# Light expert stages spread over eight heavy blocks, and light activations turned as one block diagonal tile

## The reference

```python
def _moe(h, router, w_gate, w_up, w_down):      # cut to what matters
    logits = xf @ router
    top_logits, top_idx = lax.top_k(logits, 2)
    gates = softmax(top_logits)
    # rows of each expert, padded to blocks
    y = silu(xb @ w_gate[e]) * (xb @ w_up[e]) @ w_down[e]     # 1024 x 3584, 1024 x 3584, 3584 x 1024
    out = segment_sum(y * slot_gate, slot_tok)
```

## Time and profile before

| | us |
|---|---|
| median of 3 executions | 1515.26 (1514.31 to 1519.34) |
| the profiled execution | 1516.86 |
| its span, first to last instruction | 1515.0 |
| TensorE busy | 1476.6 (97% of the span) |
| VectorE, ScalarE, GpSimd busy | 911.1, 734.3, 302.9 |

### The profile page before, as it was taken

How to read it: one execution, slowest core, us unless ns; L and a number is a source line. 1 busy time by engine, 2 the same in 40 slices (tenths; PEclk the granted TensorE clock), 3 DMA queues, 4 the chain that set the end, 5 groups by cost and what they waited for, 6 DMA issues and landing times.

```text
span 1515.0 us, 22445 instructions
## 1 busy us (share of the span) xinstructions
PE 1476.6 (97%) x9550; PEld 1133.6 (75%) x9550; DVE 911.1 (60%) x665; ACT 734.3 (48%) x588; POOL 302.9 (20%) x295
## 2 busy tenths in 40 slices
PE   9999999999999999999999999999999999999997
PEld 8887889999998878886666666667666666666785
DVE  6555665655556866885555546555555555555686
ACT  5444455344336435774444445444444544444565
POOL 5599324500024401880000000000000000000100
PEclk9999999999999999999999999999999999999999
DMA  9645538765531164999999999999999999999993
GB/s 346 190 161 173 172 134 299 276 232 190 182 129 42 47 259 150 374 392 407 394 410 403 398 409 413 411 408 408 407 401 397 410 402 409 407 394 407 409 396 150
DMA packets 141597, 469.61 MB, mean 310 GB/s; under 512 B 8648, under 2 KB 21152, under 8 KB 129200
## 3 DMA queue, kind: packets, MB, share of 16 engines
q1 hardware_dynamic: 137424, 454.58, 78.3%
q0 software_dynamic: 3920, 13.44, 2.7%
q10 hardware_dynamic: 144, 0.07, 0.0%
HBM read 462.02 MB, written 15.21 MB: 315 GB/s over the span
## 4 chain that ended last, share of the span: by engine, by line
PE 73%; DMA 14%; DVE 6%; ACT 4%; issue 1%; POOL 1%; POOLq 0%; SPq 0%; ACTq 0%; DVEq 0%
PE PS L2066 70%; DMA weights_raw<-in_moe_w_up 8%; DVE weights_lo L1560 4%; DMA weights_raw<-in_moe_w_gate 4%; ACT weights_hi L1132 3%; PE PS L2281 1%; DMA row_back<-results_by_slot,pair_index 1%; DMA weights_raw<-in_moe_w_down 1%; POOL b_padded L950 1%; PE PS L2480 1%; ACT c_padded L1132 0%; DMA results_by_slot<-small_expert_rows 0%; DVE residual L1560 0%; DMA constants<-in_constants 0%; DVE residual L1955 0%
## 5 line engine op out<-in xcount | busy, mean ns | idle before, releaser
L1560 DVE TENSOR_TENSOR weights_lo<-weights_raw,weights_hi 128x2048 fp32r<-128x2048 f32 (+2 forms) x323 | 680.2, 2117 | 406.4 <-ACT weights_hi L1132 405.3
L1132 ACT ACTIVATE weights_hi<-weights_raw 128x2048 fp32r<-128x2048 f32 (+2 forms) x323 | 564.7, 1754 | 465.2 <-PE PS L2066 311.2
L2066 PE MATMUL PS<-weights_hi,gathered_hi 128*128 128x512 f32 (+1 forms) x640 | 240.2, 375 | 1.6 <-DVE weights_lo L1560 1.0
L2066 PE MATMUL PS<-weights_hi,gathered_lo 128*128 128x512 f32 (+1 forms) x640 | 234.5, 366 | 0.0
L2066 PE MATMUL PS<-weights_lo,gathered_hi 128*128 128x512 f32 (+1 forms) x640 | 234.2, 366 | 0.0
L2066 PE MATMUL PS<-weights_hi,act_transposed_hi 128*128 128x512 f32 x456 | 185.9, 408 | 2.3 <-DVE weights_lo L1560 2.3
L2066 PE MATMUL PS<-x_transposed_hi,weights_hi 128*128 128x256 f32 x640 | 181.2, 283 | 1.3 <-DVE weights_lo L1560 1.1
L2066 PE MATMUL PS<-weights_hi,act_transposed_lo 128*128 128x512 f32 x456 | 180.6, 396 | 0.0
L2066 PE MATMUL PS<-weights_lo,act_transposed_hi 128*128 128x512 f32 x456 | 180.0, 395 | 0.0
L2066 PE MATMUL PS<-x_transposed_hi,weights_lo 128*128 128x256 f32 x640 | 179.6, 281 | 0.0
L2066 PE MATMUL PS<-x_transposed_lo,weights_hi 128*128 128x256 f32 x640 | 179.6, 281 | 0.0
(11 more groups left out here) (330 smaller groups left out, 1453.4 us busy)
## 6 DMA issues: line engine op xcount, KB each, us to landing
weights_raw<-in_moe_w_up SPq DMA_DIRECT2D x127, 896.0 KB, 9.7
weights_raw<-in_moe_w_gate SPq DMA_DIRECT2D x125, 896.0 KB, 9.6
weights_raw<-in_moe_w_down SPq DMA_DIRECT2D x96, 1024.0 KB, 8.3
weights_raw<-in_ret_w_in SPq DMA_DIRECT2D x24, 1024.0 KB, 6.6
weights_raw<-in_moe_w_down SPq DMA_DIRECT2D x32, 512.0 KB, 9.0
weights_raw<-in_ffn_w_gate SPq DMA_DIRECT2D x14, 1024.0 KB, 5.1
weights_raw<-in_ffn_w_up SPq DMA_DIRECT2D x14, 1024.0 KB, 5.1
weights_raw<-in_ffn_w_down SPq DMA_DIRECT2D x14, 1024.0 KB, 4.9
```

Source lines behind the costliest of these rows:

```text
L1132: return nc.scalar.activation(o, i, ACT.Copy)
L1560: return nc.vector.tensor_tensor(o, a, b, op)
L2066: return nc.tensor.matmul(o, l, r, start=start, stop=stop)
```

## The change

It does three things.

1. A light stage stands over eight heavy blocks each time: behind blocks 1, 2, 3, 4, 6 and 7 of eight. The first is still behind k = 16; the last moves from k = 104 to k = 110, behind unit i = 29 of `LAST`.
2. The light activations get a tile of 896 columns in which token half t holds its own 448 columns, so silu and the product are two instructions of 64 partitions each. TensorE turns it with 7 full 128x128 transposes instead of 14 products of 64x64, in two parts (4 and 3) between the units of the next two heavy blocks, and ScalarE copies each part out in two instructions. The second part of the transposes waits for the first part's copies. The tile lies where the last spare weight buffer was.
3. The four `add_back` steps stand ahead of units i = 36, 38, 40, 42 instead of 30, 33, 36, 39.

```diff
@@ small_positions
         for at in range(6):
             after[k] = 6 * stage + at
-            k += 2 if at == 3 else 1
-        k += stage % 2
+            k += 2 if at in (3, 5) else 1
@@ tiles
-        act_small = place("small_act_rows", [HALF_EC], F32, K_OFF + 9984)
+        act_small = place("small_act_rows", [EC], F32, H_OFF + 24576)
+        small_halves = [(slice(SMALL_SLOTS * h, SMALL_SLOTS * (h + 1)), slice(HALF_EC * h, HALF_EC * (h + 1))) for h in range(2)]
+        small_parts = (slice(0, 4), slice(4, EFT))
@@ ScalarE, after_small_turn
-                    act.wait_ge(turned_small, ESTEPS * LIGHT.index(q) + s + 1)
-                    copy(act_t_small[:, :, :], PS[:, 6, 0:HALF_EC].rearrange("p (f c) -> p f c", f=EFT)).then_inc(act_small_ready, 1)
+                    for part, tiles in enumerate(small_parts):
+                        act.wait_ge(turned_small, 2 * done + part + 1)
+                        rows = PS[:, 6, :].rearrange("p (f c) -> p f c", c=P)
+                        for t, _ in small_halves:
+                            ins = copy(act_t_small[t, tiles, :], rows[t, 0:tiles.stop - tiles.start, t])
+                        ins.then_inc(act_small_ready, 1)
@@ VectorE
-                        if q == LAST and i in (30, 33, 36, 39):
-                            add_back(0, (i - 30) // 6, (i - 30) // 3 % 2)
+                        if q == LAST and i in (36, 38, 40, 42):
+                            add_back(0, (i - 36) // 4, (i - 36) // 2 % 2)
@@ TensorE, turn_small
-                    for ft in range(EFT):
-                        for t in small_tile:
-                            ins = mm(PS[t, 6, ft * SMALL_SLOTS:(ft + 1) * SMALL_SLOTS], act_small[t, ft:HALF_EC:EFT], ident[t, t],
-                                     True, True)
+                    if half:
+                        pe.wait_ge(act_small_ready, 2 * done + 1)
+                    else:
+                        pe.wait_ge(mult_small, done + 1)
+                    tiles = small_parts[half]
+                    for ft in range(tiles.start, tiles.stop):
+                        c = slice((ft - tiles.start) * P, (ft - tiles.start + 1) * P)
+                        ins = nc.tensor.transpose(PS[:, 6, c], act_small[:, ft:EC:EFT], ident)
```

More of the change, by code:

```diff
@@ L1456, in after_small @@
                     if done:
-                        act.wait_ge(turned_small, done)
-                    nc.scalar.activation(act_small[:, :], PS[:, 6, 0:HALF_EC], ACT.Silu).then_inc(silu_small, 1)
+                        act.wait_ge(turned_small, 2 * done)
+                    for t, c in small_halves:
+                        ins = nc.scalar.activation(act_small[t, c], PS[t, 6, 0:HALF_EC], ACT.Silu)
+                    ins.then_inc(silu_small, 1)
                 elif kind == "down" and s == ESTEPS - 1:
@@ L1472, in after_small_turn @@
                 if kind == "up" and part:
-                    act.wait_ge(turned_small, ESTEPS * LIGHT.index(q) + s + 1)
-                    copy(act_t_small[:, :, :], PS[:, 6, 0:HALF_EC].rearrange("p (f c) -> p f c", f=EFT)).then_inc(act_small_ready, 1)
+                    done = ESTEPS * LIGHT.index(q) + s
+                    for part, tiles in enumerate(small_parts):
[4 more added lines that the diff above has]
+                        ins.then_inc(act_small_ready, 1)
             def first_pass():
@@ L1976, in after_small @@
                     dve.wait_ge(used, done_at(NUMBER[q, 2 * b + 1]))
-                    tt(act_small[:, :], act_small[:, :], PS[:, 6, 0:HALF_EC], ALU.mult).then_inc(mult_small, 1)
+                    for t, c in small_halves:
+                        ins = tt(act_small[t, c], act_small[t, c], PS[t, 6, 0:HALF_EC], ALU.mult)
+                    ins.then_inc(mult_small, 1)
             def first_pass():
@@ L2311, in _, with turn_small @@
             small_tile = [slice(SMALL_SLOTS * h, SMALL_SLOTS * (h + 1)) for h in range(2)]
-            def turn_small(j):
+            def turn_small(j, half):
                 q, b = block_of(LIGHT, j)
@@ L2334, in small_block @@
                 if kind == "down" and part == 0:
-                    pe.wait_ge(act_small_ready, done + 1)
+                    pe.wait_ge(act_small_ready, 2 * done + 2)
                     if s == 0 and q > LIGHT[0]:
@@ L2679, in first_pass, with between @@
                         turn_small_slots(LIGHT[0])
-                    j, last_j = small_after(k), small_after(k - 1)
+                    j = small_after(k)
+                    def between():
+                        for half in range(2):
+                            if small_after(k - 1 - half) is not None:
+                                turn_small(small_after(k - 1 - half), half)
                     expert_block(b, lambda i: NUMBER[q, i], STEPS + ESTEPS * at, half0=None if at else half0, n_out=at or None,
                                  turn_next=put_back if q == LAST else lambda: turn_landed(16 * TURNS.index(WHOLE[at + 1])),
-                                 ends=q == LAST, between=None if last_j is None else lambda: turn_small(last_j))
+                                 ends=q == LAST, between=between)
                     if j is not None:
```

2 lines of the change are left out of this document (1 added, 1 removed).

## The result

| us | before | after |
|---|---|---|
| median of 4 executions | 1516.08 (1514.31 to 1519.34) | 1536.94 (1534.27 to 1537.25) |
| the profiled execution | 1516.86 | 1534.27 |
| its span | 1515.0 | 1532.5 |

After is slower: 1.0131 of before, with a 95% interval of 1.011 to 1.0152. The forecast was 1523 with a range from 1517 to 1529, so the direction was right and the size was not: +20.9 us, where about +7.5 was forecast.

A forecast was written before the change was run, and what follows sets the result against it. Loads were taken to bound the kernel up to 1470 us, then TensorE. 1449.5 + 25 + 35.9 = 1510.4 against 1503.4, +7.0, plus 0.5 for the clock: span 1522.5, median about 1523, range 1517 to 1529.

The forecast's parts named there:

- Where the last light block ends: Six more heavy blocks ahead of the last light block move its end by 27.0 us of loads, from 1422.5 to 1449.5.
- rival 3: ScalarE is held by the second part of the turn, in 12 stages: up to +3 us, about 1526; chance 0.05.
- T: End of the last light block in the profiled execution: 1422.5 us before, 1457.6 after; forecast 1449.5.
- The 27.0: Load time of six heavy blocks, 11.01 MB at 408 GB/s, taken as the least the last light block's end could move.
- The turn: Light transposes save 0.75 us in each of 12 stages, 9 us of TensorE, worth 0; added ScalarE and VectorE work hidden, 0.
- The landing: The last `row_back` gather lands 25 us after the last light block, between a floor of 22 and a ceiling of 29.4.
- The stall: TensorE waits about 12 us at unit 36, whose low part stands behind VectorE's first addition, which waits for the gathers.
- Landing to end: From the gathers' landing to the end of the weight products: 35.9 us, with VectorE behind through additions and low parts.
- the clock: TensorE's granted clock falls to 0.50 in the stall, costing 0 to 2.9 us afterwards; 0.5 taken.
- What is behind the weights: Scatter, norm and store behind the last weight product: 11.6 us, unchanged.
- M: Experiments' rival: TensorE's time for light and heavy turns at the meeting places, not ScalarE's copy, costs; no chance given.

The follow-up runs named there:

- y_order: After, with only ScalarE's copies of the light turn's second part moved one unit later, behind a high part: 1527.90 us, 1.0067 of before.
- y_all: After, with own buffer for light slot rows, additions at units 42, 44, 46 and behind 47, second part's copies one unit later: 1509.30 us, 0.9944 of before.
- x_late: After, with the four additions moved to units 42, 44, 46 and behind the last low part: 1524.89 us, 1.0051 of before.
- b_pos_slots: Before, keeping its old turn, with eight-block positions, late additions and a separate buffer for light slot rows: 1520.58 us, 1.0023 of before.
- x_slots: After, with a separate buffer for the light experts' slot rows: 1534.11 us, 1.0113 of before.

## Why the prediction was right or wrong

- *Where the last light block ends.* **This step failed.** It had 1449.5, "since the DMA was never short of work"; measured 1457.6, 8.1 later. The DMA was short of work, several times, because raw buffers were freed late; it had been so, more mildly, in before, where a mean share of 1.02 hid it. I had seen the copy that waits (rival 3) but weighed it against TensorE's slack, at up to 3 us and 0.05. The thing to weigh it against was the release of the six raw buffers: where a late high part lets the queue of loads run dry, a stretch that the loads bound doesn't get that time back. Not every us of wait does so: the order took 14.0 us of the copies' waits away in `y_order` and 7.3 of T. Two mechanisms share the loss, ScalarE's order (7.3 alone) and the slot rows (5.5 once the other is mended), 12.8 in all, more than the 8.1 missed. The 27.0 as "no less" was also wrong: `y_all` needs 22.3 (1444.8 - 1422.5), its DMA at 408 GB/s where before had 405. Before had lost time of the same kind (its 11 holes; `y_all` has six). The sign given for rival 3, that TensorE's waits in the middle name ScalarE or VectorE, would have missed it: they name weight loads and the slot rows, and VectorE for 2.2 us only. Those for down weights grew from 0.7 to 5.1 us, that for the slot rows from 0 to 5.4.
- *The turn.* "Worth 0" on TensorE's side can't be told apart. Priced for ScalarE and VectorE by the length of the copies, it was "hidden, 0"; it cost 12.8 us at the old positions. That this is the copies' waits there too (32.6 us) was not tested at these positions; at the new ones the order of the copies alone was worth 9.0.
- *The landing.* Forecast 25 after that block, measured 25.5 (1483.1 - 1457.6). Bounded by 22 and 29.4, it came where it was put, and mostly for the reason given: with fewer loads beside it (2.15 MB from 13.4 to 29.4 us behind the block, where it was 4.54) the last gather took 10.1 us where it took 12.9. The other 1.1 of the 3.9 us is that it was issued 15.4 us after the block and not 16.5, since the issue ahead of it was short (below), which the sum did not use. `x_late`, with the loads going on, has 12.8 and 29.4 again.
- *The stall.* Forecast 12, measured 12.5 (VectorE) and 12.49 (TensorE, at 1486.58); taking it away gave 12.0 and 12.2. The addition, covered before, held up TensorE at unit 36 as forecast.
- *Landing to end.* Forecast 35.9 and 0.5 for the clock; measured 37.8, of which the clock 1.1. The other 0.8 was not tracked down.
- *What is behind the weights.* Forecast unchanged at 11.6; it was (1520.9 to 1532.5).

The forecast's +7.5 for the span, with 8.1 (last light block), 0.5 (landing) and 1.4 (landing to end) added, is the 17.5 us by which the spans differ. The medians differ by 20.9; after's other executions have spans of 1535.1 to 1535.5, and where they spend the rest was not profiled, so some 3 us of the median's miss stay open.

Open is what the positions cost with the old turn (`b_pos_slots`, 8 us of T). The old turn's 1.85 us on TensorE (from 1372.80) stand one unit ahead of the heavy turn there, which begins at 1377.15; in after the first part takes 0.41 (from 1372.77) and the heavy turn begins at 1375.47. That fits the wait of 3.47 us in place of 1.96, and M; it was not tested by itself.

The idea of the change was sound: in `y_all` T to the end of the weight products is 51.2 us (1444.8 to 1496.0) where it was 80.9 (1422.5 to 1503.4). That is 29.7 gained for 22.3 given, 7.4 us net. The medians differ by 7.4 (1516.72 to 1509.30), the profiled spans by 6.6 (1515.0 to 1508.4).

## What to carry to other kernels

In a stretch that the loads bound, an engine's added work is not free just because the engine is half idle: where engines go through fixed lists and free the buffers that loads wait for, the place of each wait in a list counts, so follow every added wait to the release of a buffer and look for holes in the DMA rate in windows of 5 us. When work is moved, move with it whatever waits for its result (here the additions), and look at each single buffer that it shares with work that stays (here the slot rows). Two holds can mask each other, so that mending one shows nothing: try both together before a cause is dismissed. And a mean that reads full can hide both.

## What the runs showed of the hardware

The gathers' issues on GpSimd grew short once VectorE stopped. In after, VectorE is idle from 1470.6 (1468.57 + 2.02):

```profile
1469.36 2.08 POOL L1073 DMA_INDIRECT row_back<-results_by_slot,pair_index  x1 [0.30 <-issue]
1471.75 0.94 POOL L1073 DMA_INDIRECT row_back<-results_by_slot,pair_index  x1 [0.30 <-issue]
1472.99 0.93 POOL L1073 DMA_INDIRECT row_back<-results_by_slot,pair_index  x1 [0.31 <-issue]
```

In `x_late`, the same kernel but for the places of the additions, VectorE goes on making low parts, and the last of the four issues takes 2.15 us:

```profile
1475.37 2.15 POOL L1073 DMA_INDIRECT row_back<-results_by_slot,pair_index  x1 [0.30 <-issue]
```

The rule that the prediction named from the Trainium skill ("SBUF — State Buffer", section "SBUF: two separate sides"), that the two engines exclude each other at this port, fits: 0.93 against 2.15 us. So do the ends of the slow issues: after's first two end at 1469.06 and 1471.44, 0.91 and 0.85 us behind the end of the low part that ran when they began (1468.15 and 1470.59), which is about what a short issue takes.

TensorE's clock fell in the stalls. In after its last product ahead of the long one ends at 1474.1 (1486.58 - 12.49), and it starts again at 1486.6. The granted clock is 1.00 (2.4 GHz) in 1474 to 1476, 0.51 in 1476 to 1478, 0.50 (1.2 GHz) up to 1488, 0.58 in 1488 to 1490 and 1.00 behind that. Around the wait of 5.4 us for the slot rows (923.3 to 928.7) it is 1.00 in 925 to 926, 0.74 in 926 to 927, 0.50 up to 933, 0.84 in 933 to 934 and 1.00 in 935 to 940. In `x_slots`, without that wait, it is 1.00 over 923 to 935.
